# Five boundary edits in a two-block transformer kernel on one core

## The chip, the cores and the metric

The kernel runs on one core of a Trainium2 chip. The metric is device time in microseconds (us) from launch to the end; less is better. The time before is the median of three runs.

## The reference, cut to what matters

Everything is float32, 512 tokens by 1024 features. The first block normalises x, projects it with one wide matrix, runs an mLSTM branch and a stick-breaking attention branch, gates both, multiplies by w_out and adds to x; then it applies an MLP. The second block normalises, projects, runs three attention branches (compressed, selected, window) that are summed under gates, multiplies by nsa_w_out, normalises the product and adds it.

```python
z = jnp.einsum('bqhd,bshd->bhqs', q[:, t0:t1], k[:, :t1]) * scale      # stick_breaking
suffix = lax.cumsum(log_keep, axis=3, reverse=True) - log_keep
A = jnp.where(strict, jnp.exp(jax.nn.log_sigmoid(z) + suffix), 0.0)
...
x = x + y.astype(x.dtype) @ w_out[l]                                   # first block, after the mixers
h2 = rms_norm(x, norm_mlp_g[l])
x = x + jnp.square(jax.nn.relu(h2 @ w_up[l])) @ w_down[l]
...
u = rms_norm_2(h, pre_norm_gain[layer])                                # second block
zs = jax.nn.silu(z).reshape(B, S, 3, H, dh)                            # in nsa_mixer
y = jnp.sum(gates * o * zs, axis=2).reshape(B, S, NSA_WIDTH)
h = h + rms_norm_2(y @ w_out, post_norm_gain[layer])
```

## The kernel before, in words

One program, five engines, all orders written out by hand and tied by counting semaphores. x stays in SBUF as x_sb, four blocks (b or j, 0 to 3) of 128 tokens by 1024 columns; its transposed, normalised form is act_hi and act_lo, eight feature tiles k.

Every wide float32 product is made of three fp32r products. A weight slab (1 MB, 128 partitions by 2048) is loaded by SyncE's DMA queue (SP) into one of two w_raw buffers; ACT rounds it into w_hi (split_hi, L666), DVE takes the rest into w_lo (split_lo, L674), each with two places chosen by n % 2, and PE multiplies in mm_tile (L697) or mm_half (L720). Each tile is 24 matmuls; a half slab gives 12 of them to each of four tiles. split_hi(n) waits until slab n - 2 has been used; a load waits until the slab that was in its buffer has been split. Tiles go to PSUM banks ps_g (two) and ps_z (two of its three), and act_evacuate and dve_evacuate empty them. The slabs run in one list: N_VB to N_VB + 3 (values of the stick-breaking branch), N_OA to N_OA + 7 (output gates), N_GA, N_GB, N_WO (w_out), four quarters of the MLP from N_MLP, N_NQ and the other projections of the second block, N_ZW (last branch's wide gates), N_NO (nsa_w_out) up to N_ALL.

**Stick-breaking heads.** For each head h PE computes scores into ps_z (L1368), the value product of head h - 1 (L1354), the gate tile 0 of slab N_OA + h and the first half of its tile 1 (SB_CUT = 4 of eight k), then the suffix sums (L1379 to L1392), which need sp_hi and sp_lo, then the rest of tile 1. ACT makes Abs, Exp and Ln of the scores (L1782 to L1784), DVE, GpSimd (POOL) and ACT the mask and the split (L2124, L2416, L1789, L2128), DVE the minimum on the diagonals (L2134) and ACT the last Exp (L1794), which the scores of head h + 1 wait for. Head 0's scores stand behind all four tiles of slab N_VB + 3.

**Norms.** Where the residual is complete, ACT squares a block and sums it (L1007), DVE makes the mean (L1029), ACT the root (L1015), DVE the reciprocal and the scaled block xn (L1036, L1041), and PE turns it into eight feature banks (feature_tiles, L748), which ACT and DVE copy into act_hi (L808) and act_lo (L819, L821). Norm 1 stands before the MLP, norm 2 before N_NQ; norm 3's place only turns o_a. The parts of a norm are blocks 0 and 1 together, then 2, then 3.

**MLP end.** Each quarter makes seven products (M1, M2, M6, M5, M7, M3, M4 in this order) and DVE adds them to quarters of x_sb (L2214): M1 and M2 to the left columns of blocks 0 and 1, M6 and M3 to the right columns of these, M5 and M7 to the right columns of blocks 2 and 3, M4 to their left columns; M3 is the last for blocks 0 and 1, M4 for 2 and 3. Their weights wait in four down_raw buffers.

**The end.** The last slab's four tiles are squared by ACT with a sum (L889), scaled by DVE into y2 (L977); DVE adds the two halves' sums (L2400) and makes the mean (L2401), ACT the root (L1977), DVE the reciprocal (L2403) and the output block xo (L2405), which SP sends out (L1213).

Of the kernel before, what the change touches and what calls it, by code (L numbers as in the profile page):

```python
# [163 lines left out]
def program(nc, a, out):  # L164

    with ExitStack() as ctx:
# [71 lines left out]

        qn = sb("qn", [P, 8, S], at=arena)
# [37 lines left out]
        ssq = sb("ssq", [P, 4, TB])  # L277
        rstd = sb("rstd", [P, 4, TB])
# [377 lines left out]

        def split_hi(act, n):

            if n >= N_ALL:
                return  # L660
            b = n % 2
            wait_raw(act, n)
            if n >= 2:

                wait_slab_used(act, n - 2)
            nc.scalar.activation(slab_view(w_hi[b], n), slab_view(raw(n), n), ACT.Copy).then_inc(hi_done, 1)  # L666

        def split_lo(dve, n):

            if n >= N_ALL:  # L670
                return
            b = n % 2
            dve.wait_ge(hi_done, n + 1)
            nc.vector.tensor_tensor(slab_view(w_lo[b], n), slab_view(raw(n), n),  # L674
                                    slab_view(w_hi[b], n).bitcast(F32), ALU.subtract).then_inc(lo_done, 1)

        def mm_tile(pe, n, i, hi=act_hi, lo=act_lo, ks=range(KT), activation_ready=None):
# [3 lines left out]
            b, w = n % 2, slabs[n][3]  # L681
# [3 lines left out]
            for k in ks:  # L685
                if activation_ready is not None and i == 0:
                    activation_ready(k)
                if kind in FEATURE:
                    o = bank(t)
                    three = ((w_hi[b][:, k, m], hi[:, k, :]), (w_hi[b][:, k, m], lo[:, k, :]),  # L690
                             (w_lo[b][:, k, m], hi[:, k, :]))
                else:
                    o = bank(t)[:, 0:w]
                    three = ((hi[:, k, m], w_hi[b][:, k, 0:w]), (hi[:, k, m], w_lo[b][:, k, 0:w]),
                             (lo[:, k, m], w_hi[b][:, k, 0:w]))
# [129 lines left out]
        def act_evacuate(act, n, i):  # L825
# [65 lines left out]
            elif kind == "zw":  # L891
# [5 lines left out]
                nc.scalar.activation(ev_t[:, g, :], bank(t), ACT.Tanh, scale=0.5).then_inc(ev_act, 1)  # L897
# [3 lines left out]
        def dve_evacuate(dve, order, n, i):  # L901
# [63 lines left out]
            elif kind == "zw":  # L965
# [33 lines left out]

        NORM_PARTS = (((0, 4),), ((0, 2), (2, 3), (3, 4)), ((0, 2), (2, 3), (3, 4)))  # L1000
# [3 lines left out]
        def act_square(act, which, j, block_there):  # L1004
# [3 lines left out]
            if j + 1 in [part[1] for part in NORM_PARTS[which]]:  # L1008
                ins.then_inc(sq_done, 1)

        def act_root(act, which, p):
# [3 lines left out]
            nc.scalar.activation(rstd[:, which, j0:j1], ssq[:, which, j0:j1], ACT.Sqrt).then_inc(std_ready, 1)  # L1015

        def act_rms(act, which, block_there):

            for p, (j0, j1) in enumerate(NORM_PARTS[which]):
                for j in range(j0, j1):  # L1020
                    act_square(act, which, j, block_there)
                act_root(act, which, p)

        def dve_mean(dve, which, p):
# [3 lines left out]
            v = ssq[:, which, j0:j1]  # L1028
            nc.vector.tensor_scalar(v, v, 1.0 / D, EPS, ALU.mult, ALU.add).then_inc(var_ready, 1)  # L1029
# [88 lines left out]
        def _(sp):  # L1118
# [92 lines left out]
            for b in range(TB):  # L1211
                sp.wait_ge(out_ready, b + 1)
                sp.dma_start(out_rows[:, b, :], xo[:, b, :]).then_inc(out_done, 16)  # L1213
            sp.wait_ge(out_done, 16 * TB)
# [3 lines left out]
        def _(pe):  # L1218
# [121 lines left out]
            for n in range(N_VB + 1, N_VB + 4):  # L1340
                mm_slab(pe, n)

# [15 lines left out]
            for h in range(HB):  # L1358
# [13 lines left out]
                if h:  # L1372
                    sb_values(h - 1)
                mm_tile(pe, n, 0)
# [271 lines left out]
        def _(act):  # L1646
# [118 lines left out]
            for n in range(N_VB + 1, N_VB + 4):  # L1765
                act_slab(act, n)

# [4 lines left out]
            for h in range(HB):  # L1772
                n = N_OA + h
                split_hi(act, n + 1)
# [10 lines left out]
                if h:  # L1785
                    sb_out(h - 1)
                for p, part in enumerate(SP_PARTS):
# [828 lines left out]
```

## Time and profile before

| | |
|---|---|
| median of three runs | 1329.74 us (1329.05 to 1330.46) |
| the profiled execution's own time | 1325.25 us |
| its span, first to last instruction | 1323.5 us |
| granted TensorE clock, mean | 0.997 |
| PE busy | 1300.4 us, 98% |
| DVE, ACT, POOL busy | 773.5, 683.5, 196.6 us |
| HBM traffic | 98 GB/s over the span |

The engines are PE (TensorE), PEld (its weight loads), DVE (VectorE), ACT (ScalarE), POOL (GpSimd) and SPq (SyncE's DMA queue). A busy PE is one with matmuls in flight. L697 is line 697 of the kernel before. A duration overlaps the next instruction's start a little, so two starts tell more than one duration.

### The profile page before, as it was taken

Reading aid. Unit: us, or ns where it says so; the run is one execution under the profiler, and the core shown is the slowest. Engines: PE = TensorE matmul, PEld = TensorE weight load, DVE = VectorE, ACT = ScalarE, POOL = GpSimd, SP = SyncE. Lnnn points to the kernel's source line nnn. Section 1 sums busy time; section 2 is a strip of 40 time slices with the busy share of each in tenths; the row PEclk is TensorE's granted clock in tenths of the full one; section 3 lists DMA queues with packets and bytes.
Section 4 is the critical chain, followed back from the end, with each engine's and each line's share of the span. In section 5 each row is a group of like instructions: output and inputs, shape, how many; then the busy total and the mean of one; then the engine's idle time right before and its main releaser. Section 6 shows DMA issues by size and latency. Waiting matters only on the chain.

```text
span 1323.5 us, 16610 instructions
## 1 busy us (share of the span) xinstructions
PE 1300.4 (98%) x6548; PEld 1062.7 (80%) x6548; DVE 773.5 (58%) x1197; ACT 683.5 (52%) x1051; POOL 196.6 (15%) x260
## 2 busy tenths in 40 slices
PE   8999999999999999999999999999999999999998
PEld 6787777777778887888888888788898888888876
DVE  5873443345454545595775958821256778777564
ACT  5535555446766434553635546544244677675242
POOL 0102333151000000000000000003612333431000
PEclk9999999999999999999999999999999999999999
DMA  7522222373111234234070430372612232231311
GB/s 256 149 94 96 92 93 72 102 217 94 41 57 64 80 111 141 83 125 130 0 242 13 149 106 0 96 227 80 142 33 63 68 102 71 68 102 57 112 64 63
DMA packets 66988, 130.98 MB, mean 99 GB/s; under 512 B 3983, under 2 KB 36751, under 8 KB 63072
## 3 DMA queue, kind: packets, MB, share of 16 engines
q1 hardware_dynamic: 60864, 111.07, 25.1%
q0 software_dynamic: 5904, 18.81, 5.6%
q8 instruction: 52, 0.85, 0.3%
q14 instruction: 24, 0.20, 0.1%
q10 hardware_dynamic: 144, 0.06, 0.0%
HBM read 127.04 MB, written 2.88 MB: 98 GB/s over the span
## 4 chain that ended last, share of the span: by engine, by line
PE 92%; DVE 3%; ACT 2%; DMA 1%; issue 1%; POOL 0%; SPq 0%; DVEq 0%; ACTq 0%
PE ps_g L697 40%; PE ps_g L720 14%; PE ps_z L720 7%; PE ps_t L1438 6%; PE ps_z L1438 5%; PE ps_z L1549 3%; PE ps_z L1587 3%; PE ps_t L1621 3%; PE ps_t L1316 1%; PE ps_t L1354 1%; PE ps_z L1368 1%; PE ps_t L1471 1%; DMA x_sb<-in_x 1%; PE ps_z L1392 1%; ACT w_hi L666 1%
## 5 line engine op out<-in xcount | busy, mean ns | idle before, releaser
L697 PE MATMUL ps_g<-act_hi,w_hi 128*128 128x512 f32 x784 | 309.6, 395 | 3.6 <-DVE act_lo L821 1.8
L674 DVE TENSOR_TENSOR w_lo<-w_raw,w_hi 128x2048 fp32r<-128x2048 f32 (+1 forms) x82 | 186.1, 2269 | 213.9 <-ACT w_hi L666 213.6
L697 PE MATMUL ps_g<-act_hi,w_lo 128*128 128x512 f32 x784 | 306.1, 390 | 0.0
L697 PE MATMUL ps_g<-act_lo,w_hi 128*128 128x512 f32 x784 | 305.9, 390 | 0.0
L666 ACT ACTIVATE w_hi<-w_raw 128x2048 fp32r<-128x2048 f32 (+1 forms) x82 | 155.3, 1894 | 89.3 <-PE ps_g L720 52.1
L697 PEld LDWEIGHTS ps_g<-act_hi,w_hi 128*128 128x128 f32 x784 | 147.6, 188 | 36.5 <-issue 4.8
L697 PEld LDWEIGHTS ps_g<-act_hi,w_lo 128*128 128x128 f32 x784 | 147.6, 188 | 31.4
L697 PEld LDWEIGHTS ps_g<-act_lo,w_hi 128*128 128x128 f32 x784 | 147.7, 188 | 29.7
L720 PE MATMUL ps_g<-w_hi,act_hi 128*128 128x512 f32 x240 | 96.7, 403 | 0.7 <-DVE act_lo L819 0.7
L720 PE MATMUL ps_g<-w_hi,act_lo 128*128 128x512 f32 x240 | 93.7, 390 | 0.0
L720 PE MATMUL ps_g<-w_lo,act_hi 128*128 128x512 f32 x240 | 93.3, 389 | 0.0
L2509 POOL TENSOR_SCALAR cmp_in_k<-pairk,vec 128x124 f32<-128x124 f32 x16 | 11.7, 745 | 492.6 <-ACT pairk L876 492.6
L1910 ACT ACTIVATE probs<-probs,rneg 128x128 f32<-128x128 f32 (+3 forms) x128 | 70.4, 552 | 7.9 <-DVE rneg L2330 7.7
L666 ACT ACTIVATE w_hi<-down_raw 128x2048 fp32r<-128x2048 f32 x24 | 46.0, 1918 | 52.4 <-PE ps_t L1438 30.7
L2529 POOL TENSOR_TENSOR q_parts<-qn,q_parts 64x512 fp32r<-64x512 f32 x32 | 41.9, 1310 | 120.6 <-ACT q_parts L1890 120.1
L674 DVE TENSOR_TENSOR w_lo<-down_raw,w_hi 128x2048 fp32r<-128x2048 f32 x24 | 55.0, 2290 | 8.0 <-ACT w_hi L666 8.0
L858 ACT ACTIVATE ev_t<-ps_g 128x512 f32<-128x512 f32 x32 | 19.1, 596 | 75.0 <-PE ps_g L697 75.0
L2326 DVE CUSTOM_DVE_ANT_0 probs<-ps_z,tile_t 128x128 f32<-128x128 f32 (+3 forms) x128 | 55.0, 485 | 3.2 <-PE ps_z L1549 3.2
L720 PEld LDWEIGHTS ps_g<-w_hi,act_lo 128*128 128x128 f32 x240 | 45.0, 188 | 9.8
L720 PEld LDWEIGHTS ps_g<-w_hi,act_hi 128*128 128x128 f32 x240 | 45.1, 188 | 9.2 <-issue 1.1
L720 PEld LDWEIGHTS ps_g<-w_lo,act_hi 128*128 128x128 f32 x240 | 45.2, 188 | 8.4
L947 DVE TENSOR_TENSOR up_lo<-up_raw,up_hi 128x256 fp32r<-128x256 f32 (+1 forms) x32 | 17.8, 557 | 55.1 <-ACT up_hi L863 55.1
(372 smaller groups left out, 2524.0 us busy)
## 6 DMA issues: line engine op xcount, KB each, us to landing
w_raw<-in_w_in_t SPq DMA_DIRECT2D x30, 1024.0 KB, 4.8
w_raw<-in_nsa_w_in SPq DMA_DIRECT2D x22, 1024.0 KB, 5.1
w_raw<-in_w_up SPq DMA_DIRECT2D x16, 1024.0 KB, 5.5
down_raw<-in_w_down SPq DMA_DIRECT2D x16, 1024.0 KB, 5.3
tile_t<-bias_rev_dram POOLq DMA_DIRECT2D x32, 256.0 KB, 3.1
bc<-stat_rows_dram POOLq DMA_DIRECT2D x24, 256.0 KB, 6.2
w_raw<-in_w_out SPq DMA_DIRECT2D x4, 1024.0 KB, 5.1
w_raw<-in_nsa_w_out SPq DMA_DIRECT2D x4, 1024.0 KB, 5.0
```

What stands on the lines that cost most here:

```text
L666: nc.scalar.activation(slab_view(w_hi[b], n), slab_view(raw(n), n), ACT.Copy).then_inc(hi_done, 1)
L674: nc.vector.tensor_tensor(slab_view(w_lo[b], n), slab_view(raw(n), n), slab_view(w_hi[b], n).bitcast(F32), ALU.subtract).then_inc(lo_done, 1)
L697: mm = nc.tensor.matmul(o, stationary, moving, start=(k == 0 and j == 0), stop=(k == KT - 1 and j == 2))
L720: mm = nc.tensor.matmul(bank(t), act[:, k, m], w[:, k - k0, :], start=(k == 0 and j == 0), stop=(k == KT - 1 and j == 2))
L858: nc.scalar.activation(ev_t[:, g, :], ps_g[:, g, :], ACT.Relu).then_inc(ev_act, 1)
L1438: mm = nc.tensor.matmul(down_bank(p, i), act[:, k, m], w[:, k, :], start=(first and k == 0 and j == 0), stop=(k == HALF_K - 1 and j == 2), ...
L1549: mm = nc.tensor.matmul(ps_z[:, at:at + w], q_parts[u % 2][:, b * P:(b + 1) * P], keys[u // 4 % 2][:, 0:w], start=(j == 0), stop=(j == 1))
L1587: mm = nc.tensor.matmul(ps_z[64 * e:64 * e + 64, CAUSAL + at * P:CAUSAL + 2 * P], values[:, s, g * DH:(g + 1) * DH], blocks[:, first:last: ...
L1621: mm = nc.tensor.transpose(ps_t[:, at:at + P], probs[u % 2][:, ROWS_AT[b] + s * P:ROWS_AT[b] + (s + 1) * P], ident)
L1910: ins = nc.scalar.activation(p, p, ACT.Exp, bias=rneg[:, u % 2, b:b + 1], accum_out=rsum[:, u % 2, b:b + 1])
L2326: ins = nc.vector.tensor_tensor_reduce(probs[u % 2][:, at:at + w], ps_z[:, at:at + w], tile_t[u % 2][:, S - w:S], 1.0, -3.0e38, ALU.add, A ...
L2529: nc.gpsimd.tensor_tensor(q_parts[u % 2][64 - half:128 - half, :], qn[half:half + 64, 4 * (h // 8) + h % 4, :], q_parts[u % 2][half:half + ...
```

## The change

1. **Scores ahead of a value tile.** PE computes head 0's scores after three of the four tiles of slab N_VB + 3 and the fourth tile behind them. ACT calls an Exp on one element ahead of the head, evacuates the fourth tile behind the Ln, and in head 0 alone the split of slab N_OA + 1 moves on ACT and DVE from ahead of the head to behind sp_hi and sp_lo.
2. **Halved square sums.** Norms 1 and 2 square each block in two halves of 512 columns. For norm 1 the left halves are squared one slab earlier; for norm 2 the left halves of blocks 0 and 1 before the split of M4's slab and the right halves of blocks 2 and 3 behind the split of slab N_NQ. The mean becomes one addition of both sums, with the division in the root.
3. **A place of its own for a slab's parts.** Slab N_NQ's two parts go to first_q, 16 KB at the place of down_raw 2 and 3, so its split waits for the last split out of these and not for slab N_NQ - 2's products. DVE makes the low part in two halves between the additions of M3, and the order of additions, means and xn at the end of the MLP changes.
4. **Silu gates.** The last branch's gates of the N_ZW slabs are a Silu with two DVE operations in place of a Tanh with three.
5. **The end.** The first half of the last square sums is prepared once; ACT's root takes the second half and that bias directly, so DVE's L2400 and L2401 go. The last output block is written and sent in two halves.

```diff
+        first_q = [sb(f"first_q_{part}", [P, KT, SLAB], F32R, at=arena + 4 * K16 + 8192 * e)
+                   for e, part in enumerate(("hi", "lo"))]
...
+        def parts(n):
+            return first_q if n == N_NQ else (w_hi[n % 2], w_lo[n % 2])
         def split_hi(act, n):
...
+            if n == N_NQ:
+                act.wait_ge(lo_done, N_NQ - PRODUCTS + M3 + 1)
+            elif n >= 2:
                 wait_slab_used(act, n - 2)
...
+        def split_lo_part(dve, n, part):
+            (hi, lo), ks = parts(n), slice(part * HALF_K, (part + 1) * HALF_K)
+            dve.wait_ge(hi_done, n + 1)
+            ins = nc.vector.tensor_tensor(lo[:, ks, :], raw(n)[:, ks, :], hi[:, ks, :].bitcast(F32), ALU.subtract)
+            if part:
+                ins.then_inc(lo_done, 1)
...
-                nc.scalar.activation(ev_t[:, g, :], bank(t), ACT.Tanh, scale=0.5).then_inc(ev_act, 1)
+                nc.scalar.activation(ev_t[:, g, :], bank(t), ACT.Silu).then_inc(ev_act, 1)
...
-                order.link(nc.vector.scalar_tensor_tensor(e, e, 1.0, ps, ALU.add, ALU.mult))
-                if s == 0:
-                    order.link(nc.vector.tensor_tensor(e, e, o_b[:, i, cols], ALU.mult))
-                else:
-                    order.link(nc.vector.tensor_tensor(e, e, o_w[i // 2][:, i % 2, :], ALU.mult))
+                o = o_b[:, i, cols] if s == 0 else o_w[i // 2][:, i % 2, :]
+                order.link(nc.vector.scalar_tensor_tensor(e, e, 2.0, o, ALU.mult, ALU.mult))
                 nc.vector.tensor_tensor(o_a[:, i, cols], o_a[:, i, cols], e, ALU.add).then_inc(done, 1)
...
+        OUT_PARTS = [(slice(0, D),)] * (TB - 1) + [(slice(0, WIDE), slice(WIDE, D))]
+        def act_square(act, which, j, c, block_there):
             block_there(j)
-            ins = nc.scalar.activation(xn[j][:], x_sb[:, j, :], ACT.Square, accum_out=ssq[:, which, j:j + 1])
+            cols = slice(c * WIDE, (c + 1) * WIDE)
+            first = j // 2 if which == 2 else 0
+            sums = ssq_first[:, which - 1, j:j + 1] if c == first else ssq[:, which, j:j + 1]
+            ins = nc.scalar.activation(xn[j][:, cols], x_sb[:, j, cols], ACT.Square, accum_out=sums)
...
+            nc.scalar.activation(r, r, ACT.Sqrt, scale=1.0 / D).then_inc(std_ready, 1)
...
+            nc.vector.scalar_tensor_tensor(rstd[:, which, j0:j1], ssq_first[:, which - 1, j0:j1], EPS * D,
+                                           ssq[:, which, j0:j1], ALU.add, ALU.add).then_inc(var_ready, 1)
...
 # PE
-            for n in range(N_VB + 1, N_VB + 4):
+            for n in (N_VB + 1, N_VB + 2):
                 mm_slab(pe, n)
+            for i in (0, 1, 2):
+                mm_half(pe, N_VB + 3, i)
...
                 if h:
                     sb_values(h - 1)
+                else:
+                    mm_half(pe, N_VB + 3, 3)
 # ACT
+            split_hi(act, N_OA)
+            for i in (0, 1, 2):
+                act_evacuate(act, N_VB + 3, i)
+            order.link(nc.scalar.activation(rstd[0:1, 3, 0:1], cst[0:1, C_ID:C_ID + 1], ACT.Exp))
...
-                split_hi(act, n + 1)
+                if h:
+                    split_hi(act, n + 1)
...
                     sb_out(h - 1)
+                else:
+                    act_evacuate(act, N_VB + 3, 3)
...
                     nc.scalar.copy(sp_hi[:, part], sp_t[:, part]).then_inc(b_hi, 1)
+                if h == 0:
+                    split_hi(act, n + 1)
...
+                if n == N_WO + 2:
+                    for b in range(TB):
+                        act_square(act, 1, b, 0, lambda b: wait_tile_free(act, tile_of[N_WO + 1] + b))
...
                 for p in range(M2, PRODUCTS):
+                    if q == 3 and p == M3:
+                        for b in (0, 1):
+                            first_square(b)
+                    split_hi(act, n + 4 + p + 1)
                     if q == 3 and p == M4:
-                        last_square(0)
-                    split_hi(act, n + 4 + p + 1)
+                        for b in (2, 3):
+                            first_square(b)
...
+            last_square(0)
             last_square(1)
...
                     if n == N_ALL - 1:
-                        act.wait_ge(var_ready, parts_before(3) + i + 1)
-                        r = rstd[:, 3, i:i + 1]
-                        nc.scalar.activation(r, r, ACT.Sqrt).then_inc(std_ready, 1)
+                        act.wait_ge(var_ready, parts_before(3) + 1)
+                        after_act(act, tile_of[n] + i, 1)
+                        nc.scalar.activation(rstd[:, 3, i:i + 1], ssq_y[:, i, 1:2], ACT.Sqrt, scale=1.0 / D,
+                                             bias=ssq[:, 3, i:i + 1]).then_inc(std_ready, 1)
 # DVE
+                if h == 0:
+                    split_lo(dve, n + 1)          # behind sp_lo; ahead of the head only for h > 0
...
                             add_product(q, p - 1, i)
+                            if q == 3 and p == M4:
+                                split_lo_part(dve, N_NQ, i)
...
             dve_mean(dve, 2, 0)
-            add_product(3, M4, 0)
             dve_inverse(dve, order, 2, 0)
             dve_normed(2, 0)
+            add_product(3, M4, 0)
+            dve_normed(2, 1)
             add_product(3, M4, 1)
             dve_mean(dve, 2, 1)
-            dve_normed(2, 1)
             dve_inverse(dve, order, 2, 1)
...
+            nc.vector.tensor_scalar(ssq[:, 3, :], ssq_y[:, :, 0], 1.0 / D, EPS, ALU.mult, ALU.add)\
+                .then_inc(var_ready, 1)
             for b in range(TB):
                 dve_evacuate(dve, order, N_ALL - 1, b)
                 r = rstd[:, 3, b:b + 1]
-                order.link(nc.vector.tensor_reduce(r, ssq_y[:, b, 0:2], AX_X, ALU.add))
-                nc.vector.tensor_scalar(r, r, 1.0 / D, EPS, ALU.mult, ALU.add).then_inc(var_ready, 1)
                 dve.wait_ge(std_ready, parts_before(3) + b + 1)
                 order.link(nc.vector.reciprocal(r, r))
                 wait_tile_free(dve, tile_of[N_ALL - 1] + b)
-                nc.vector.scalar_tensor_tensor(xo[:, b, :], y2[:, b, :], r, x_sb[:, b, :],
-                                               ALU.mult, ALU.add).then_inc(out_ready, 1)
+                for c in OUT_PARTS[b]:
+                    nc.vector.scalar_tensor_tensor(xo[:, b, c], y2[:, b, c], r, x_sb[:, b, c],
+                                                   ALU.mult, ALU.add).then_inc(out_ready, 1)
```

## Rows read from the trace of the kernel before

**Rows 1.** The page, its first part: busy us (share of the span) by engine.

```profile
PE 1300.4 (98%) x6548; PEld 1062.7 (80%) x6548; DVE 773.5 (58%) x1197; ACT 683.5 (52%) x1051; POOL 196.6 (15%) x260
```

**Rows 2.** PE's waits: for whom, us in total, times, longest.

```profile
PE ps_z L748 <- DVE xn L1041: 2.1, 3, 1.1
...
PE ps_z L1385 <- DVE sp_lo L2128: 1.5, 1, 1.5
PE ps_z L1379 <- DVE sp_lo L2128: 0.9, 1, 0.9
```

**Rows 3.** Chain that ended last, heads 0 and 1: start, us, what.

```profile
278.37 5.45 PE ps_g L720 x24
...
299.86 2.80 PE ps_g L697 x12
302.66 2.16 PE ps_z L1368 x8
...
306.98 8.22 PE ps_g L697 x36
...
317.92 2.80 PE ps_g L697 x12
```

**Rows 4.** Timeline of ACT, 228 to 322 us: start, us, instruction, [idle before].

```profile
281.13 0.60 ACT L842 ACTIVATE v_b<-ps_g 128x512 f32<-128x512 f32 x1 [2.12 <-PE ps_g L720]
...
286.14 1.24 ACT L1782 ACTIVATE sp_t<-ps_z 128x1280 f32<-128x1280 f32 x1
287.39 1.28 ACT L1783 ACT_TABLE_LOAD   x1
...
300.83 1.24 ACT L1794 ACTIVATE attn_b<-ps_z 128x1280 f32<-128x1280 f32 x1 [2.62 <-DVE ps_z L2134]
```

**Rows 5.** Timeline of DVE, heads 0 and 1.

```profile
296.33 0.96 DVE L2128 TENSOR_TENSOR sp_lo<-sp_t,sp_hi 128x768 fp32r<-128x768 f32 x1 [1.29 <-ACT sp_hi L1789]
...
313.90 0.96 DVE L2128 TENSOR_TENSOR sp_lo<-sp_t,sp_hi 128x768 fp32r<-128x768 f32 x1 [1.29 <-ACT sp_hi L1789]
```

**Rows 6.** Timeline of PE, norm 1: transposes into ps_g.

```profile
520.75 1.19 PE L748 MATMUL ps_g<-cst,xn 128*128 128x128 f32 x8
```

**Rows 7.** Timeline of PE, end of the MLP and norm 2.

```profile
849.87 0.39 PE L1438 MATMUL ps_t<-w_hi,up_lo 128*128 128x512 f32 x1
...
853.52 0.49 PE L748 MATMUL ps_z<-cst,xn 128*128 128x128 f32 x3
...
854.18 1.04 PE L748 MATMUL ps_g<-cst,xn 128*128 128x128 f32 x8
```

**Rows 8.** Timeline of DVE, end of the MLP and norm 2.

```profile
847.39 2.29 DVE L674 TENSOR_TENSOR w_lo<-w_raw,w_hi 128x2048 fp32r<-128x2048 f32 x1 [1.86 <-ACT w_hi L666]
...
851.13 0.68 DVE L2214 TENSOR_TENSOR x_sb<-x_sb,ps_t 128x512 f32<-128x512 f32 x1
...
853.31 0.15 DVE L1029 TENSOR_SCALAR ssq<-ssq 128x1 f32<-128x1 f32 x1
...
853.93 0.88 DVE L1041 TENSOR_SCALAR xn<-x_sb,rstd 128x512 f32<-128x512 f32 x2
```

**Rows 9.** Timeline of PE, the turning of o_a (norm 3's place).

```profile
1270.05 0.49 PE L748 MATMUL ps_g<-cst,o_a 128*128 128x128 f32 x3
1271.11 0.76 PE L748 MATMUL ps_g<-cst,o_a 128*128 128x128 f32 x5 [0.57 <-DVE o_a L974]
```

**Rows 10.** Timeline of DVE, 1257 to 1323.5 us.

```profile
1270.36 0.69 DVE L974 TENSOR_TENSOR o_a<-o_a,ev_t 128x512 f32<-128x512 f32 x1
...
1318.41 0.14 DVE L2400 TENSOR_REDUCE rstd<-ssq_y 128x1 f32<-128x2 f32 x1
...
1319.01 0.16 DVE L2403 RECIPROCAL rstd<-rstd 128x1 f32<-128x1 f32 x1 [0.27 <-ACT rstd L1977]
1319.21 1.28 DVE L2405 SCALAR_TENSOR_TENSOR xo<-y,rstd,x_sb 128x1024 f32<-128x1024 f32 x1
```

**Rows 11.** DMA issues, 1300 to 1324 us: KB each, median us to landing.

```profile
out_dram<-xo SPq DMA_DIRECT2D x4, 512.0 KB, 2.6
```

More of the change, by code:

```diff
@@ L660, in split_hi @@
                 return
-            b = n % 2
             wait_raw(act, n)
-            if n >= 2:
+            if n == N_NQ:
+                act.wait_ge(lo_done, N_NQ - PRODUCTS + M3 + 1)
+            elif n >= 2:
                 wait_slab_used(act, n - 2)
-            nc.scalar.activation(slab_view(w_hi[b], n), slab_view(raw(n), n), ACT.Copy).then_inc(hi_done, 1)
+            nc.scalar.activation(slab_view(parts(n)[0], n), slab_view(raw(n), n), ACT.Copy).then_inc(hi_done, 1)
         def split_lo(dve, n):
@@ L1002, in parts_before @@
             return sum(len(parts) for parts in NORM_PARTS[:which])
-        def act_square(act, which, j, block_there):
+        def act_square(act, which, j, c, block_there):
             block_there(j)
-            ins = nc.scalar.activation(xn[j][:], x_sb[:, j, :], ACT.Square, accum_out=ssq[:, which, j:j + 1])
-            if j + 1 in [part[1] for part in NORM_PARTS[which]]:
+            cols = slice(c * WIDE, (c + 1) * WIDE)
+            first = j // 2 if which == 2 else 0
+            sums = ssq_first[:, which - 1, j:j + 1] if c == first else ssq[:, which, j:j + 1]
+            ins = nc.scalar.activation(xn[j][:, cols], x_sb[:, j, cols], ACT.Square, accum_out=sums)
+            if c != first and j + 1 in [part[1] for part in NORM_PARTS[which]]:
                 ins.then_inc(sq_done, 1)
@@ L1014, in act_root @@
             act.wait_ge(var_ready, parts_before(which) + p + 1)
-            nc.scalar.activation(rstd[:, which, j0:j1], ssq[:, which, j0:j1], ACT.Sqrt).then_inc(std_ready, 1)
+            r = rstd[:, which, j0:j1]
+            nc.scalar.activation(r, r, ACT.Sqrt, scale=1.0 / D).then_inc(std_ready, 1)
         def act_rms(act, which, block_there):
@@ L1020, in act_rms @@
                 for j in range(j0, j1):
-                    act_square(act, which, j, block_there)
+                    act_square(act, which, j, 1, block_there)
                 act_root(act, which, p)
@@ L1210, in _ @@
             out_rows = out.rearrange("(b p) n -> p b n", p=P)
[L1211 to L1214, printed above, removed]
+            parts = [(b, c) for b in range(TB) for c in OUT_PARTS[b]]
+            for n, (b, c) in enumerate(parts):
+                sp.wait_ge(out_ready, n + 1)
+                sp.dma_start(out_rows[:, b, c], xo[:, b, c]).then_inc(out_done, 16)
+            sp.wait_ge(out_done, 16 * len(parts))
         @block.tensor
@@ L1764, in _ @@
             nc.scalar.activation(stats[:], stats[:], ACT.Sqrt).then_inc(stat_roots, 1)
-            for n in range(N_VB + 1, N_VB + 4):
+            for n in (N_VB + 1, N_VB + 2):
                 act_slab(act, n)
+            split_hi(act, N_OA)
+            for i in (0, 1, 2):
+                act_evacuate(act, N_VB + 3, i)
+            order.link(nc.scalar.activation(rstd[0:1, 3, 0:1], cst[0:1, C_ID:C_ID + 1], ACT.Exp))
             def sb_out(h):
@@ L1819, in copy_product, with first_square @@
                 nc.scalar.copy(prod1[:, i, :], down_bank(M1, i)).then_inc(prod_copied, 1)
+            def first_square(b):
+                act_square(act, 2, b, b // 2, lambda b: act.wait_ge(first_added, 2 * 3 + b + 1) if b < 2 else
+                           act.wait_ge(prod_added, added(3, M7, b - 2)))
             def last_square(b):
-                act_square(act, 2, b, lambda b: wait_rows(act, 3, b))
+                act_square(act, 2, b, 1 - b // 2, lambda b: wait_rows(act, 3, b))
             for q in range(4):
@@ L2241, in _ @@
                             add_product(q, M1, i)
-                    split_lo(dve, n + 4 + p + 1)
+                    if n + 4 + p + 1 < N_NQ:
+                        split_lo(dve, n + 4 + p + 1)
                     if p == M2:
```

23 lines of the change are left out of this document (12 added, 11 removed).

## The prediction, made blind

> **What bounds the kernel now.** I read the page first: PE is busy for 98% of the span [rows 1]. Time can therefore only come from work that PE no longer does, and this change leaves all its products in place, or from stretches in which PE stands. The second view is PE's list of waits [rows 2]. It says who keeps it standing: the square and norm chain at two norms, and the low part of the log terms in stick-breaking head 0 (0.9 and 1.5 us, once each). The third view is the chain that ended last, because a busy PE can hide a slow one. Head 0 runs from the end of the last value tile at 278.37 + 5.45 = 283.82 to the second half of gate tile 1 at 299.86, that is 16.04 us. Head 1 takes 317.92 - 302.66 = 15.26 us for the same, and 2.16 of it (304.82 to 306.98) are the value product that head 0 lacks, so 13.10 [rows 3]. Head 0 is 2.94 us over PE's own work. Last come the timelines around each boundary, for the order of events.
>
> The sum is made against the profiled execution, whose own time is 1325.25 us (span 1323.5 and 1.75 around it). The median of the runs is 4.49 above it, and I carry the difference over to the median. A change under 0.2% (2.7 us) can't be told from none here.
>
> **1. Scores ahead of the value tile.** Nothing is added on PE: eight score matmul groups and a 12-matmul half tile change places. The scores start one half tile (5.45 / 2 = 2.72) earlier, at 281.10, and the half tile now stands between them and the suffix sums. ACT: the table load of 1.28 in front of the Exp [rows 4] goes to 281.73, behind the third tile's evacuation (281.13 + 0.60), and ends at 283.03; the one-element Exp ends near 283.25. Scores end at 283.26, so Abs starts at about 283.4. Before, Abs started at 286.14, since the split of slab N_OA + 1 stood ahead of it, and the last sp_lo ended at 296.33 + 0.96 = 297.29 [rows 4, 5]: 11.15 us, less the 1.28 load 9.87, so 293.3 now. PE gets there at 281.10 + 2.16 + 2.72 + 8.22 = 294.20, 0.9 later. Both waits close, and the gain is the whole 2.94.
> What is pushed back: ACT's split now ends near 294.1 and DVE's (2.29, as the one in [rows 8]) near 296.3, then the gate tile and the diagonal minimum (some 1.5 us), then the last Exp (1.24) until 299.1. PE needs it at 281.10 + 2.16 + 2.72 + 8.22 + 2.72 + 2.80 = 299.72. The next slab load on SP's queue starts 7.7 us later and is wanted two heads (36 us) later. The fourth tile's evacuation waits behind the Ln until 289; PE wants its bank at 291.3. If the preload were not hidden, sp_lo would be 0.4 late and the gain 2.5; if the last Exp slipped by 1.5 as well, 1.5. I take 2.94, bounds 1.5 and 2.94.
> The load is also where the skill weighs in. The row has 1.28 us from the load to the next instruction and no drain [rows 4]. The Trainium skill (ScalarE: Activation LUTs, What ACT_TABLE_LOAD costs) gives about 2.66 us for a switch with its drain. By its figure the preload would end at 284.4, sp_lo near 294.5 and the gain would be 2.6, not 2.94.
>
> **2. Halved squares.** Norm 1: eight more ACT calls; the four early ones lie in ACT's idle time between two slab splits. DVE adds block 3's last columns only once PE is done, and block 2's xn stands behind that, so nothing of that moves. Block 3's xn comes some 0.4 earlier, but PE stands only little for it: eight transposes took 1.19 us here and 1.04 in norm 2, where nothing was late [rows 6, 7]. Gain 0.15; bounds 0 and 0.4.
>
> **3. Slab N_NQ's own place, and the order at the MLP's end.** Before, PE ended its last product at 849.87 + 0.23 = 850.10 and began block 2's transposes at 853.52 [rows 7]. DVE was splitting N_NQ until 849.68 [rows 8]; only then came the first mean, the additions of M4 and the xn. Now ACT can split N_NQ behind M4's slab, near 841.3 to 843.1 (its load was issued at 833.15 and takes 5.3), and DVE cuts its low part in two halves, both out by 847.2. With the two early half squares M3's blocks have their mean near 847.3, and xn 0 and 1 are out before PE ends. DVE can add M4's second tile at 850.10 + 0.19 = 850.29. From there: the addition 0.60 (0.68 less its overlap), mean to xn 853.93 - 853.31 = 0.62 with the root between, so block 2's xn starts at 851.51 and is out 0.8 later [rows 8]. PE turns blocks 0 and 1 meanwhile (16 transposes of 0.11) and starts block 2 at 852.31, not 853.52: gain 1.21. Block 3's xn is due at 853.3 and PE gets to it at 853.6, so what follows keeps its length. Were PE never late it would be 1.68; if N_NQ's weights held ACT, so that DVE's halves delayed M3's addition, 0.5 or less. I take 1.21.
>
> **4. Silu gates.** One DVE operation of three goes from behind the last gate tile. It costs 1270.36 to 1271.11 = 0.75 with its hand-over [rows 10], and 0.73 from start to start. PE's own transposes last until 1270.05 + 3 x 0.11 = 1270.38, and it went on at 1271.11 [rows 9]. So all but nothing of the 0.73 counts: 0.70. One more table load of 1.28 [rows 4] falls at the first gate tile some 30 us ahead, in ACT's idle time. On the path it would make this edit -0.6.
>
> **5. The end.** DVE's two small operations and the way to ACT and back stand between 1318.41 and the reciprocal at 1319.01 [rows 10]. ACT's root is now done by 1318.1, before y2, so the reciprocal follows at 1318.41: 0.60 earlier. The two half blocks take as long as the whole. The last transfer carries half the bytes. 512 KB land in 2.6 us [rows 11]; half could save from nothing to 1.3, and I take the middle, 0.65, less nothing for the issue, since the first half's is over when the second is ready. Sum 1.25. If the two transfers got in each other's way and the second took 1.0 longer, the edit would be -0.4.
>
> **Sum.** 2.94 + 0.15 + 1.21 + 0.70 + 1.25 = 6.25 us. Profiled execution 1325.25 - 6.25 = 1319.0; median 1329.74 - 6.25 = **1323.5 us**. The bad ends together: 1.5 + 0 + 0.5 - 0.6 - 0.4 = 1.0 (1328.7); the good ends: 2.94 + 0.4 + 1.68 + 0.73 + 1.9 = 7.65 (1322.1).
>
> **The rivals.** *Part of it only*: the chain in head 0 or the MLP's end stays late, or the halved transfer gives nothing. For it: both rest on several engines being on time within 0.3 to 0.9 us. Against: each has a reckoned margin. With 1.5 for edit 1, 0.8 for edit 3 and 0.6 for edit 5 the sum is 3.75, so 1326.0.
> *Nothing to be told*: what is won at a boundary is lost at the next wait, because a later event hangs on something that does not move. For it: the steady head has little room, as sp_lo ends at 313.90 + 0.96 = 314.86 and PE wants it at 306.98 + 8.22 = 315.20 [rows 3, 5]. Against: everything behind a boundary is released by PE, ACT or DVE, which all move with it. Gain 1.0, 1328.7.
> *Slower: the heads lose their table sets.* Heads 1 to 7 need no load for either Exp, since the set that holds Tanh serves it: head 0's last Exp at 300.83 has none [rows 4]. If with the new Exp and Silu calls the loads were placed otherwise, each head would get two more, 1.28 ahead of the first Exp and 1.28 ahead of the last. The room is 0.34 for the first (315.20 - 314.86) and 0.59 for the second (302.66 less 300.83 + 1.24) [rows 3 to 5], so a head would be 0.94 + 0.69 = 1.63 longer, seven heads 11.4, and the time 1323.5 + 11.4 = 1334.9. It decides for slower from (6.25 + 2.7) / 7 = 1.3 us a head. Against: the order of functions inside heads 1 to 7 isn't touched.
> The Trainium skill (ScalarE activation tables: per-element evaluation and per-set limits, Table sets in the compiler and the runtime) says that loads are placed per block by the greedy longest run; no run here has shown yet what new calls do to that.
>
> **How the numbers follow.** The forecast 0.63, part only 0.23, nothing to be told 0.09, slower 0.05. The likeliest case spans 1322.1 to 1325.0. The range takes in the part case and a median's own spread of 0.7 (the three runs) below: **1321.2 to 1327.0**, with the two last cases and the far ends left out. Faster is the forecast and the part case with a little off its end: 0.87; same 0.09; slower 0.04.
>
> **What would show it.** Edit 1: no wait of PE for sp_lo, and second half of gate tile 1 at about 296.9. If it fails, the table load stands again at the first Exp or PE waits for attn_b. Edit 2: eight transposes in 1.04 at norm 1. Edit 3: split of N_NQ near 841, block 2's transposes 2.2 after the last product. It is wrong if that split waits for its load. Edit 4: PE stands for no o_a. Edit 5: the last xo ends 0.6 earlier and its transfer lands under 2.6. The whole is wrong if the heads' period of 18.06 us (302.66 on) grows, or a table load appears in it.

## The result: 1319.7 us, and a cause that the sum did not hold

The changed kernel takes 1319.68 us in the median of 4 runs (1318.85 to 1321.55), the kernel before on the same chip 1329.39 us (4 runs, 1327.83 to 1330.46). The ratio is 0.9938, its 95% interval 0.9924 to 0.9952. The forecast was 1323.5 us with a range from 1321.2: the direction was right, but the time came out below the range.

Nearly all of the path went as forecast. The two profiles start differently, so they are compared from one event on: the first wide product behind the start, PE's 24 matmuls into ps_z at 87.2 us before. This is the tile view of ps_z around it in the changed kernel (count, ns of one, first and last start):

```profile
L738 PE MATMUL ps_z<-w_hi,act_hi x8: 389/389/389, 89.7 to 94.5; 128*128 128x512 f32 x8
```

From there to the end it is 1319.8 - 89.7 = 1230.1 us, before 1323.5 - 87.2 = 1236.3: 6.2 us less, where the sum has 6.25. So the start was 2.5 us later in this one execution, and that is why its own time is no lower than 1321.55. The trace shows where it lost them: PE stands 2.42 us for a weight slab's low part ahead of 43.87, and right behind this wait the granted clock is 0.66 over 5 us. Around it, changed kernel (us of the span; busy us of PE, PEld, DVE, ACT and POOL with the count, then PEclk, the granted clock, DMA share, GB/s):

```profile
43.87 0.50 PE L715 MATMUL ps_g<-act_hi,w_hi 128*128 128x512 f32 x1 [2.42 <-DVE w_lo L683]
45.00:50.00 5.00, 5.00 (x17) 3.94 (x16) 3.43 (x3) 3.77 (x4) 3.79 (x4) 0.66 0.98 272
```

The chain that ended last, heads 0 and 1 [for rows 3]:

```profile
283.65 2.16 PE ps_z L1391 x8
285.81 2.77 PE ps_g L738 x12
288.58 8.16 PE ps_g L715 x36
...
299.45 2.78 PE ps_g L715 x12
302.23 2.16 PE ps_z L1391 x8
...
306.55 8.21 PE ps_g L715 x36
...
317.47 2.78 PE ps_g L715 x12
```

Head 0's scores stand ahead of the half tile now, and no ACT or DVE piece is in the chain. From the scores to the second half of gate tile 1 it is 299.45 - 283.65 = 15.80 us, all of it PE's own work: 2.16 + 2.77 + 8.16, and 2.71 for the suffix sums. PE's waits [for rows 2] have no sp_lo in them, and xn went from 2.1 to 1.0 us:

```profile
PE ps_z L766 <- DVE xn L1061: 1.0, 2, 0.6
```

ACT and DVE in head 0 [for rows 4 and 5]. The profile is 2.56 us late here against before, so the forecast's times are to be read 2.56 higher:

```profile
283.69 0.60 ACT L860 ACTIVATE v_b<-ps_g 128x512 f32<-128x512 f32 x1 [2.12 <-PE ps_g L738]
284.31 1.28 ACT L1795 ACT_TABLE_LOAD   x1
...
285.90 1.24 ACT L1812 ACTIVATE sp_t<-ps_z 128x1280 f32<-128x1280 f32 x1
```

```profile
294.83 0.96 DVE L2176 TENSOR_TENSOR sp_lo<-sp_t,sp_hi 128x768 fp32r<-128x768 f32 x1 [1.31 <-ACT sp_hi L1821]
```

The load starts at 284.31 (forecast 281.73 + 2.56 = 284.29), Abs at 285.90 (285.96), the last sp_lo ends at 295.79 (295.86), and PE, which would want it at 296.74, is the later one, by 0.95.

The MLP's end: DVE [for rows 8], and PE [for rows 6, 7 and 9]. PE's last product ended 0.86 us earlier than before (849.24 for 850.10).

```profile
843.37 1.22 DVE L690 TENSOR_TENSOR first_q_lo<-w_raw,first_q_hi 128x1024 fp32r<-128x1024 f32 x1
...
845.11 1.22 DVE L690 TENSOR_TENSOR first_q_lo<-w_raw,first_q_hi 128x1024 fp32r<-128x1024 f32 x1
846.24 0.15 DVE L1048 SCALAR_TENSOR_TENSOR rstd<-ssq_first,ssq 128x2 f32<-128x2 f32 x1
...
849.45 0.69 DVE L2264 TENSOR_TENSOR x_sb<-x_sb,ps_t 128x512 f32<-128x512 f32 x1 [0.57 <-PE ps_t L1463]
```

```profile
520.03 1.04 PE L766 MATMUL ps_g<-cst,xn 128*128 128x128 f32 x8
...
851.48 0.55 PE L766 MATMUL ps_z<-cst,xn 128*128 128x128 f32 x3 [0.63 <-DVE xn L1061]
...
1268.10 1.10 PE L766 MATMUL ps_g<-cst,o_a 128*128 128x128 f32 x8
```

The two halves of the slab's low part lie between M3's additions, the first mean comes before PE has ended, and DVE waits for PE at M4 (0.57) instead of PE for DVE. Norm 1's eight transposes take 1.04 now, and the eight at norm 3's place no longer stand for o_a.

The end [for rows 10 and 11], DVE and the DMA issues:

```profile
1315.15 0.69 DVE L992 TENSOR_TENSOR y<-ps_z,gain_bc 128x512 f32<-128x512 f32 x1 [0.64 <-ACT ev_t L907]
1315.76 0.15 DVE L2456 RECIPROCAL rstd<-rstd 128x1 f32<-128x1 f32 x1
1315.95 1.41 DVE L2459 SCALAR_TENSOR_TENSOR xo<-y,rstd,x_sb 128x512 f32<-128x512 f32 x2
```

```profile
out_dram<-xo SPq DMA_DIRECT2D x3, 512.0 KB, 2.6
out_dram<-xo SPq DMA_DIRECT2D x2, 256.0 KB, 2.0
```

The reciprocal follows y2 at once, the two half passes take 1.41 instead of 1.28 us, and half the bytes land in 2.0 instead of 2.6 us.

So the profiles have the forecast's 6.2 us, and the times have more: 9.7 us between these medians. The experiments were made to find the rest. The kernel before ran between them, and medians are compared on one chip. For each of their executions there is also TensorE's mean granted clock over the span, and it turned out to be of use; for the kernel before's four runs above there is none.

### The profile page after: what moved, and what is told of

Same layout as the page of the kernel before. It is cut to its first block, busy times and chain, and to the rows that moved or that the text cites. A ratio compares the mean times of both kernels' runs of the same rounds, so it can differ in the third digit from the quotient of the medians.

```text
span 1319.8 us, 16620 instructions
## 1 busy us (share of the span) xinstructions
PE 1298.4 (98%) x6548; PEld 1062.4 (80%) x6548; DVE 767.3 (58%) x1184; ACT 687.4 (52%) x1069; POOL 196.7 (15%) x260
## 4 chain that ended last, share of the span: by engine, by line
PE 94%; DVE 2%; DMA 2%; ACT 1%; issue 1%; SPq 0%; POOL 0%; DVEq 0%; ACTq 0%
PE ps_g L715 41%; PE ps_g L738 14%; PE ps_z L738 7%; PE ps_t L1463 7%; PE ps_z L1463 5%; PE ps_z L1574 3%; PE ps_z L1612 3%; PE ps_t L1646 3%; DMA w_raw<-in_w_in_t 2%; PE ps_t L1337 1%; PE ps_z L1391 1%; PE ps_t L1377 1%; PE ps_t L1496 1%; PE ps_z L1417 1%; PE ps_z L1325 1%; ACT w_hi L675 1%
## 5 line engine op out<-in xcount | busy, mean ns | idle before, releaser
L715 PE MATMUL ps_g<-act_hi,w_hi 128*128 128x512 f32 x768 | 302.9, 394 | 5.1 <-DVE w_lo L683 4.0
L715 PE MATMUL ps_g<-act_hi,w_lo 128*128 128x512 f32 x768 | 299.9, 391 | 0.0
L715 PE MATMUL ps_g<-act_lo,w_hi 128*128 128x512 f32 x768 | 299.6, 390 | 0.0
L715 PEld LDWEIGHTS ps_g<-act_hi,w_hi 128*128 128x128 f32 x768 | 144.7, 188 | 37.6 <-DVE w_lo L683 4.8
L715 PEld LDWEIGHTS ps_g<-act_hi,w_lo 128*128 128x128 f32 x768 | 144.5, 188 | 30.6
L715 PEld LDWEIGHTS ps_g<-act_lo,w_hi 128*128 128x128 f32 x768 | 144.7, 188 | 28.8
```

Of the source, the lines that this page charges most:

```text
L715: mm = nc.tensor.matmul(o, stationary, moving, start=(k == 0 and j == 0), stop=(k == KT - 1 and j == 2))
```

## Experiments

### Copies, and one part alone

```diff
 layout_only: the kernel before and
+        ssq_first = sb("ssq_first", [P, 2, TB])
 scores_only: the kernel before and the first part of the change (scores, preload, order of the splits)
```

> The kernel before, unchanged, timed against itself. Theory A (the five edits are worth some 6.2 us, and the other 3.4 of the measured 9.7 are how the first 90 us of an execution fall out, whatever the kernel): the median lies within 1.5 us of the other copy's, single runs are spread over 3 us or more, and the profile begins its 13th slab's half tile (87.36 us in the first profile) anywhere from 87 to 92 us. Theory B (the 9.7 are the change's own): all runs at 1328 to 1330.5 us, and the profile's 1325.25 was the odd one.

> The changed kernel, unchanged, timed again. Theory A: 6.2 us under the kernel before on this chip, give or take 1 (ratio 0.9953); the part behind the start is 1229.9 us long as in its first profile. Theory B: 9.7 under it again (ratio 0.9927).

> The kernel before with the 32 bytes of ssq_first reserved and never used, so that all buffers behind it stand where the changed kernel has them. Theory A: as the kernel before, within 0.7 us. Theory B in its likeliest form (the buffers' places change how early transfers or code land): 2 to 3.5 us faster.

> Edit 1 alone: head 0's scores ahead of the fourth value tile, with the Exp ahead and the moved split. Theory A: 2.9 us faster, and in the profile no wait of PE for sp_lo; head 0 takes 16.0 - 2.9 us over the same stretch. Rival (part of it only): 1.5 us. Theory B has part of the 3.4 here: 4 us or more.

Measured, on one chip, beside 1327.33 us for the kernel before (27 runs): its copy 1327.9 (ratio 0.9995, 0.9984 to 1.0006); the changed kernel's copy 1320.05 (0.9942, 0.9928 to 0.9956); the reserved place alone 1329.04 (1.0004, 0.9991 to 1.0017), so addresses do nothing that can be told; the first part alone 1324.1 (0.9973, 0.9961 to 0.9984), 3.2 us. On this chip, then, the whole change is worth 7.3 us, 1.0 over the sum, and its first part only 0.3 over its term: just outside the 5.2 to 7.2 us of theory A, far from theory B's 9.7.

The spread said more than the medians. The kernel before lay between 1324.5 and 1332.5 us, the changed one between 1319.4 and 1321.4. By mean granted clock, the kernel before's 27 runs fall apart: 18 at 0.997 with a median of 1326.3 us, 7 at 0.994 or 0.995 with a median of 1330.0, and 2 at 0.996 over 1330. An execution at 0.994 was caught in a profile, that of layout_only (1329.91 us). Its stretches around head 0 (busy us of each engine with the count, then PEclk, DMA share, GB/s):

```profile
295.00:300.00 5.00, 2.56 (x10) 1.58 (x9) 2.92 (x4) 3.01 (x4) 1.52 (x4) 0.88 0.02 7
300.00:305.00 5.00, 5.00 (x21) 4.81 (x20) 1.59 (x5) 0.37 (x2) 0.00 (x0) 0.50 0.00 0
305.00:310.00 5.00, 5.00 (x19) 3.50 (x19) 1.70 (x3) 3.51 (x4) 0.00 (x0) 0.93 0.01 2
```

TensorE is busy for 2.56 of 5 us, since it stands 0.92 and 1.52 us for sp_lo; then the granted clock is 0.50, that is 1.2 instead of 2.4 GHz. In the chain the same matmuls take longer:

```profile
299.46 1.01 PE ps_z L1386 x3
300.47 1.39 PE ps_z L1393 x6
301.85 0.75 PE ps_z L1386 x3
302.60 1.39 PE ps_z L1393 x6
303.99 3.65 PE ps_g L698 x12
307.64 2.16 PE ps_z L1369 x8
```

The twelve of gate tile 1 take 3.65 us, which took 2.80 before [rows 3]. From the first suffix sum behind the second wait to head 1's scores it is 307.64 - 299.46 = 8.18 us; at full clock it is 5.32 (heads_fit, below). That makes 2.9 us in one place; first wide product to the end is 1328.2 - 89.3 = 1238.9 us for 1236.3 before. The Trainium skill (TensorE: Matmul & The Clock Gate, What's actually happening) says that the default is the throttled state and that activity releases it; this trace agrees in so far as the half clock comes with and behind 5 us in which TensorE was busy for half, though its longest gap there is 1.52 us. The same waits in the profile of before have a granted clock of 1.00. So it happens in a part of the executions, and the theory was: the first part of the change takes away the stall and with it this fall.

The mean clock isn't a count of this fall, however. In 13 of the 18 profiles, of every kind of kernel, there is another between 34 and 50 us, ahead of all edited stages, and in all 18 the clock is at half for the last 0.6 to 4.1 us of the span, behind the last product, where it costs nothing. Two rows of before, then two of after_b:

```profile
35.00:40.00 5.00, 5.00 (x19) 4.07 (x19) 4.36 (x7) 4.31 (x6) 0.00 (x0) 0.66 0.56 210
1320.00:1323.50 3.50, 0.00 (x0) 0.00 (x0) 0.49 (x1) 0.00 (x0) 0.00 (x0) 0.50 0.37 150
```

```profile
35.00:40.00 5.00, 5.00 (x24) 4.39 (x23) 5.00 (x8) 4.28 (x9) 0.00 (x0) 0.64 0.57 210
40.00:45.00 5.00, 5.00 (x16) 3.92 (x16) 3.80 (x5) 1.89 (x2) 0.00 (x0) 0.67 0.00 0
```

In before this early fall of 3.4 us comes with PE busy throughout, behind sixteen narrow matmuls (33x16, 33.72 to 35.60 us). A single one there seems to cost nothing: the five profiles with no early fall wait 1.3 to 1.9 us for the next slab's low part at 43 us, the ten with 3.4 us of it at 34 to 41 us 0.5 at most, and the first wide product starts at 87.3 to 88.4 in the five and at 86.1 to 88.3 in the ten. The two with 6.8 us there (layout_only and after_b) start it at 89.3 and 89.8. after_b's profile has a mean clock of 0.996 with no fall behind head 0. So 0.994 holds a fall behind head 0 in the one execution that was traced, and for an untraced one at 0.996 or less this is likely, not shown. And the changed kernel's shorter end gives it some 0.0008 of mean clock for nothing (an estimate: half of 3.6 us of 1323.5 before, of 1.6 us of 1319.8 now).

### Taking the fall away without the stall, and the stall alone back

```diff
 scores_undone, scores_undone_b: the kernel after, its first part as before
 norms_undone, norms_undone_b: the kernel after, its second and third parts as before
 out_whole: the kernel after
-        OUT_PARTS = [(slice(0, D),)] * (TB - 1) + [(slice(0, WIDE), slice(WIDE, D))]
 heads_filled: the kernel before
+            def fill(pe, count):
+                for _ in range(count):
+                    nc.tensor.matmul(ps_t[:, 1024:1536], k_b[:, 0, 0:P], q_b[:, 0, :], start=True, stop=True)
...
                 mm_tile(pe, n, 1, ks=range(0, SB_CUT))
+                if h == 0:
+                    fill(pe, 4)
                 pe.wait_ge(b_lo, 2 * h + 1)
...
+                if h == 0:
+                    fill(pe, 6)
                 pe.wait_ge(b_lo, 2 * h + 2)
 heads_fit (on the kernel before), undone_fit (on scores_undone): as heads_filled, but
+                    nc.tensor.matmul(ps_t[:, 1024:1536], w_hi[N_OA % 2][:, 0, 0:P], act_hi[:, 0, :], start=True, stop=True)
```

> The kernel after the change with its first part alone undone: the scores of head 0 come again behind the last value tile, and head 0 waits 0.92 and 1.52 us for sp_lo. Theory A (the stall and the clock): the profile gives back 2.9 us as the sum had it, and in a part of the executions the granted clock falls to half right behind these waits for 6.83 us, which costs another 3.4 us, so that the times lie in two groups, near 1323 and 1326.5 us, with mean clocks near 0.997 and 0.994, and the median some 4 us over the changed kernel's. Theory B (the stall alone; what came beside the sum is the spread of the start): 1320 + 2.9 = 1323 us, the times as narrow as those of the changed kernel, and a mean clock of 0.997 or more in all of them.

> The kernel before, with 4 and 6 matmuls of 128x512 that nobody reads put into TensorE's two waits for sp_lo in head 0: 10 x 0.227 = 2.3 us of work in 2.4 us of waiting, at nothing on the path. Theory A (idle TensorE there lets the clock fall): head 0's end doesn't move in the profile, no execution has its clock at half behind head 0, and the group of times near 1329.5 us is gone: median near 1326.3 us, mean clocks of 0.996 to 0.998. Theory B (the clock's fall has another cause, or the wide spread is not the clock's): times and mean clocks spread as those of the kernel before, median 1327.5 us or a little over, for the matmuls put in.

> The kernel after the change with its second and third parts undone (whole square sums, no place of its own for the slab's parts behind norm 2); scores, Silu gates and the end as in the changed kernel. Theory A: the terms of the sum, 0.15 + 1.21 us, or as measured between the two profiles 0.16 + 1.13 = 1.3 us, and beside them in a part of the executions a clock at half for 3.41 us in norm 2, at 1.7 us each: median 1321.5 to 1322.3 us, spread wider than the changed kernel's on its upper side. Theory B (no clock effect): 1321.3 us, as narrow as the changed kernel.

> The kernel after the change with the last output block sent whole again: the prediction's 0.65 us for the halves. If the landing of a transfer of 256 KB takes nearly as long as one of 512 KB the loss is only that of half the VectorE pass, 0.5 us: 1320.5 to 1320.7 us against 1320.05, in the profile the last chain longer by 0.4 to 0.7 us.

On one chip, beside 1328.06 us for the kernel before: scores_undone 1323.08 (1322.19 to 1325.24), norms_undone 1322.09, out_whole 1320.88, heads_filled 1331.02.
```profile
296.81 5.31 PE L1346 MATMUL ps_t<-q_b,k_b 128*128 128x512 f32 x12
```

The path grew by 1241.9 - 1236.3 = 5.6 us (first wide product to the end), and the median by only 3.0. Some 2.6 us came back, which points to the clock, but doesn't show it. scores_undone went against the theory: its times don't lie in two groups, its mean clocks are 0.996 to 0.998, and it is only 3.2 us over the changed kernel of the later comparison on this chip (after_c, 1319.9), which is the path's 2.9 and little more. Both were done again with the changed kernel on the same chip and matmuls of the right length.

> The kernel before, with the two waits of head 0 filled by matmuls in one pass each (4 and 6 of 128x512 at 0.227 us; those of the run before came in two passes at 0.43 us and made the path 5 us longer). They fit into the waits, so that the path stays as it was: scores of head 1 where they were to 0.3 us. Theory A (idle TensorE lets the clock fall in a part of the executions): mean clock 0.997 or more in nearly all executions, none at 0.994 or 0.995, median 1 to 2 us under the kernel before on the same chip. Theory B (the fall has nothing to do with these waits): median and spread of the kernel before.

> The kernel after with its first part undone, and the same 4 and 6 matmuls in head 0's waits. Theory A: the stall's length stays (2.9 us), the clock no longer falls there: median 2.9 us over the changed kernel, and under that of the same kernel without the matmuls by 0.5 to 1.5 us. Theory B: the same as without the matmuls.

> The kernel after with its first part undone once more, now on one chip with the changed kernel and with its own copy whose waits are filled. Theory A: 3.5 to 4.5 us over the changed kernel, some executions with a mean clock of 0.996 or less and 3 us slower than the rest. Theory B: 2.9 us over the changed kernel.

> The kernel after unchanged, as the measure for the two copies of it in this call: 1320.1 us, mean clock 0.997 to 0.999, whichever theory holds.

Measured on one chip:

| kernel | median us (range, runs) | first wide product to the end, us | mean clocks of the runs |
|---|---|---|---|
| before | 1329.00 (1325.3 to 1331.4, 17) | 1236.3 (other chip) | 10 at 0.994 to 0.996, 7 at 0.997 |
| heads_fit | 1325.83 (1324.3 to 1328.6, 12) | 1236.2 | 12 at 0.997 to 0.999 |
| scores_undone_b | 1324.07 (1322.7 to 1324.5, 6) | 1234.6 | 5 at 0.996, 1 at 0.998 |
| undone_fit | 1322.49 (1321.1 to 1323.8, 6) | 1233.0 | 1 at 0.996, 5 at 0.997 to 0.999 |
| after_b | 1319.34 (1318.5 to 1321.6, 6) | 1230.1 | 1 at 0.996, 5 at 0.998 or 0.999 |

heads_fit in its profile: the fill ends just ahead of the suffix sums, on the timeline of PE,

```profile
294.11 1.07 PE L1346 MATMUL ps_t<-act_hi,w_hi 128*128 128x512 f32 x4
295.19 0.50 PE L1384 MATMUL ps_z<-sp_hi,tri_r 128*128 128x512 f32 x1
295.52 0.40 PE L1384 MATMUL ps_z<-sp_lo,tri_r 128*128 128x512 f32 x1
295.76 1.55 PE L1346 MATMUL ps_t<-act_hi,w_hi 128*128 128x512 f32 x6
297.44 0.62 PE L1392 MATMUL ps_z<-sp_hi,tri_r 128*128 128x384 f32 x3
```

and head 1's scores start at 302.76 for 302.66 before [rows 3]. The path is the same, TensorE does ten matmuls more that nobody reads, and the kernel is 3.2 us faster in the median (ratio 0.9980, 0.9969 to 0.9990), more than the 1 to 2 that theory A expected. The two profiled executions don't differ (1325.27 and 1325.25 us), so the gain lies in what the other executions had, and the clock accounts for most of it: the 12 runs' mean clocks average 0.9978 for 0.9960 in the 17 of before, 0.0018 of 1325 us = 2.4 us, where the mean times differ by 2.7. No theory without the clock was put forward that gives a gain here. Where in the span each untraced run had its falls isn't known: even before's seven runs at 0.997 have a median of 1327.3, against 1325.7 for heads_fit's six. The second pair says the same with fewer runs: 1.6 us between scores_undone_b and undone_fit. The former's profile caught a shorter fall in the same place:

```profile
295.00:300.00 5.00, 2.80 (x13) 2.36 (x14) 2.28 (x3) 2.71 (x3) 1.03 (x3) 0.87 0.00 0
300.00:305.00 5.00, 5.00 (x22) 4.32 (x21) 0.89 (x4) 1.36 (x2) 0.00 (x0) 0.79 0.00 2
```

0.13 and 0.21 of full clock are missing in 5 us each, 3.4 us at half clock in all, and the path is 1234.6 - 1233.0 = 1.6 us longer than with the waits filled. In the 5 profiles of kernels with the two waits unfilled there are 2 such falls behind head 0; in the 13 of kernels without these waits or with them filled there is none.

### Is it the same at norm 2, and do the last parts hold to the sum?

```diff
 norms_fit: norms_undone with
+            def block_ready(j):
+                for _ in range((8, 4, 0, 0, 0)[j]):
+                    nc.tensor.transpose(ps_z[:, 3 * P:4 * P], ident, ident)
+                pe.wait_ge(xn_ready, TB + 1 + j + 1)
 gates_end_undone: the kernel after, its fourth and fifth parts as before
```

> The kernel after with its second and third parts undone, now on one chip with the changed kernel. Theory A: 1.3 us of path, and where TensorE idles 1.11 and 0.60 us ahead of norm 2's transposes the clock falls to half in many executions, at 1.7 us each: 1.3 to 3.0 us over the changed kernel, near 2.3. Theory B (path alone): 1.3 us.

> The same kernel with 8 and 4 transposes of 128x128 of the identity matrix, which nobody reads, put into the first two waits of norm 2 (12 x 0.11 = 1.3 us of work in 1.7 us of waiting). Theory A: the path stays, the clock doesn't fall in norm 2 in the profile, and the median lies 0.5 to 1.7 us under that of the kernel without them. Theory B: the same median to 0.5 us.

> The kernel after with its last two parts undone (tanh gates with two more VectorE steps, last block whole, root of the last norm in three steps). Prediction's terms: 0.70 + 1.25 = 1.95 us over the changed kernel; as measured between the two profiles 0.72 + 1.03 = 1.75 us. No clock effect there in either theory, since TensorE's wait for o_a is 0.57 us and has a matmul stage of 50 us ahead; a median more than 3 us over the changed kernel would mean that there is one.

> The kernel after unchanged, as the measure of this call: 1319.3 to 1320.1 us.

Beside 1327.16 us for the kernel before: after_c 1319.9, norms_undone_b 1321.47, norms_fit 1322.04, gates_end_undone 1321.85. Filling norm 2's waits brought nothing (0.6 us slower, within the spread of six runs each), so norm 2 has no part in these medians that could be seen. The test was a weak one, since none of norms_undone_b's six runs, all at 0.997 or 0.998, shows that it had a fall to lose. The fall as such exists there: the profiles of scores_only and norms_undone have a granted clock of 0.66 from 850 to 855, and norms_undone's path is 1233.2 us against 1231.6 for norms_undone_b, whose clock is 1.00 there. This is scores_only:

```profile
850.00:855.00 5.00, 4.84 (x28) 4.59 (x28) 2.23 (x6) 1.80 (x5) 0.00 (x0) 0.66 0.31 111
```

How often it comes at norm 2 isn't settled: 2 of the 8 profiles of kernels in which norm 2 waits 1.11 and 0.60 us, none of the other 10, and no sign of it in the times.

## Why the prediction was wrong, point by point

**The step that failed** is the last one of the arithmetic: "The median of the runs is 4.49 above it, and I carry the difference over to the median." The difference was taken for something constant around the kernel. It holds chance of one execution: the profiled one of before had no fall behind head 0, while timed ones have it in part. In before_again, the same kernel, it is 1327.90 - 1326.38 = 1.52, and for the changed kernel 1319.68 - 1321.55 = -1.87. With the fall gone only the median could gain from it, and the sum, made inside an undisturbed execution, couldn't see it. On the chip with both pairs the books close: before to heads_fit 3.2 us (mostly the clock), heads_fit to after_b 6.5 us (6.1 in the path, 6.25 in the sum), together 9.7 us. On two other chips the difference was 7.3 us, 1.0 over the sum; there fewer of before's executions had a mean clock of 0.996 or less (9 of 27, and 4 of 11, here 10 of 17). The 9.7 us of the first comparison are of the same size; that its runs had the same cause is likely but not shown, since the clocks of before's runs there aren't known. The range missed it for the same reason: it was built from bounds of the path and from the spread of the three runs, and its good end (7.65 us) holds no term for a clock. Its lower end is 0.9 under 1322.1 where the spread named is 0.7; the result lies below either. How far the forecast misses is chance of the chip: it is 3.8 us here, but beside the 1327.33 us of the kernel before on another chip the same sum gives 1321.1 for a measured 1320.05.

**Edit 1**, 2.94 us: right as path. The second half of gate tile 1 stands at 299.45, and with 2.56 us of later start taken off at 296.89 (forecast 296.9). The wait for sp_lo is gone with 0.95 us to spare (0.9 forecast), and undoing it lengthens the path by 1233.0 - 1230.1 = 2.9 us. What the term lacked is what the stall can do besides lasting: in the medians it was worth 4.7 us on one chip (scores_undone_b over after_b), 3.15 with the waits filled, but 3.2 in scores_only and in scores_undone on the two others. The preload costs 1.28 us and the next instruction starts at once; the Trainium skill's 2.66 for a switch with its drain, cited in the prediction, isn't what this trace shows.

**Edits 2 and 3**, 0.15 + 1.21 = 1.36: right. N_NQ's first product starts 1.99 us earlier, 0.86 of it brought along, so 1.13 for edit 3, and 0.16 for edit 2 by the same reckoning. Undone, the path is 1231.6 - 1230.1 = 1.5 us longer and the median 1.6. The forecast's times of this boundary, each less the 0.86, are met to 0.05 us: halves out 846.34 (846.33), M4's addition 849.43 (849.45), block 2's transposes 851.45 (851.48), N_NQ's split from 840.44 (841.3 less 0.86).

**Edits 4 and 5**, 0.70 + 1.25 = 1.95: nearly right in sum, with one term mis-sized: 1231.8 - 1230.1 = 1.7 in the path; that the medians have 1.95 too is chance, with six runs spread over 3 us. Edit 4 gave 0.72, and its table load, 1.28 at 1235.68, lies 30 us ahead of where PE would notice, as forecast. The root gave 0.59 for the forecast 0.60: from the last y2 to the end it is 5.70 us before and 1316.8 - 1311.69 = 5.11 in out_whole. The halved transfer was put at 0.65 and is worth 5.11 - (1319.8 - 1315.15) = 0.46: it lands 0.6 earlier, and the two half passes take 0.13 longer than the whole.

**The rivals.** *Part of it only* and *nothing to be told* fell with the path's 6.2 us. *The heads lose their table sets* didn't happen: ACT's groups of table loads have 8 and 8 in the heads in both profiles, of 1283 ns, and the heads' period is 18.02 us for 18.06.

```profile
L1814 ACT ACT_TABLE_LOAD x8 | 10.3, 1283 | 0.1
L868 ACT ACT_TABLE_LOAD x8 | 10.3, 1283 | 0.1
```

No rival had the time better than forecast: all of them asked what of the gain would be lost.

## What to carry to other kernels

A profiled execution is one draw. Before a sum is carried to the median, ask why the two differ, and look at the runs' mean granted clocks: where they fall into groups the times may too, and an edit may remove a group. But read in a trace where the clock is low, since the mean also counts stretches at half clock that cost nothing. Price a wait of TensorE in a matmul kernel as its length and, if a second one follows closely, as a risk of half clock behind it; here the waits' 2.9 us had another 1.6 to 3.2 us in the medians behind them on one chip, and 0.3 on two others. A cheap test for this is to fill the wait with matmuls that nobody reads: if the kernel gets faster with more work and the same path, it points to the clock.

## What the runs showed that I had not expected

Two waits of 0.92 and 1.52 us with two matmuls between them were enough, in some executions and not in others of the same program, for 3.4 or 6.8 us at 1.2 GHz. What decides it is open; the executions differ in their start, as the first wide product at 86.1 to 89.8 us in 18 profiles shows, and part of this difference is itself an early fall of the clock. In the changed kernel's profile one wait of 2.42 us had 3.4 us at half clock behind it, in five others one of 1.3 to 1.9 us at the same place had none. Ten more matmuls made the kernel before 3.2 us faster. Two plain float32 operands of 128x512 cost two passes, 0.43 us, where the rounded parts cost one of 0.227.
